# An encoder layer with experts in tiles of 128 rows: a first expert tile made of four experts' first 32 rows, one scatter per tile, six square roots on ScalarE

## The reference

```
h = rms_norm(x, g_mix_norm);  proj = h @ w_in          # latents of q and kv, rotary key, and q, k, v of the second group
o_a = mla_mix(...)      # 8 heads: q and kv expanded from the latents, QK-norm per head, rotary part, dense softmax over 512 keys
o_b = na_mix(...)       # 8 heads: QK-norm, window of 8 x 16 grid points, bias, softmax
x = x + concat(rms_norm(o_a), rms_norm(o_b)) @ w_out
h2 = rms_norm(x, g_ffn_norm)
# hier_moe: group by top 1 of 4, then top 2 of the 4 experts in that group
eid = g_idx * EXPERTS_PER_GROUP + e_idx;  wts = pg_top * pe_top / sum(pe_top)
hid = silu(h2 @ w_gate[e]) * (h2 @ w_up[e]) * combine  # 1024 -> 256, 16 experts
x = x + sum over e of hid @ w_down[e]
```

## Time and profile before

| | us |
|---|---|
| median of 3 runs (lowest, highest) | 523.04 (521.43, 523.22) |
| the profiled execution's own time | 523.25 |
| its span | 521.4 |
| TensorE busy | 466.7 (90%) |
| VectorE, ScalarE, GpSimd busy | 219.9, 146.0, 171.6 |
| last product of the experts ends | 501.5 |

### The profile page before, as it was taken

One profiled execution on the slowest core, in us unless ns is written; L12 is line 12 of the kernel. 1 busy time (PEld: TensorE's weight loads), 2 busy tenths in 40 slices (PEclk: granted clock), 3 DMA queues, 4 the chain that ended last, 5 costly groups with the idle time before them and its releaser, 6 DMA issues. The chain is left out here.

```text
span 521.4 us, 7733 instructions
## 1 busy us (share of the span) xinstructions
PE 466.7 (90%) x2848; PEld 229.7 (44%) x2848; DVE 219.9 (42%) x688; ACT 146.0 (28%) x332; POOL 171.6 (33%) x175
## 2 busy tenths in 40 slices
PE   4999999989999999999999989349999999999940
PEld 2554544444555565554555556233333433333200
DVE  1222864424655645455466666435222332222110
ACT  2301422324554566544353542200111000000100
POOL 1211168878199920000010202300172222222332
PEclk9999999999999999999999999559999999999985
DMA  7999900003300000193000549965899999999312
GB/s 285 431 366 405 370 3 1 1 0 123 140 2 1 0 1 1 30 413 123 1 1 1 202 169 370 394 216 194 296 341 391 393 392 378 372 374 363 72 26 33
DMA packets 29609, 100.05 MB, mean 192 GB/s; under 512 B 5376, under 2 KB 6912, under 8 KB 29184
## 3 DMA queue, kind: packets, MB, share of 16 engines
q1 hardware_dynamic: 21216, 84.04, 41.6%
q0 software_dynamic: 5904, 8.43, 7.0%
q10 hardware_dynamic: 2448, 7.04, 3.6%
HBM read 77.39 MB, written 35.21 MB: 216 GB/s over the span
## 5 line engine op out<-in xcount | busy, mean ns | idle before, releaser
L1301 PE MATMUL bank<-arena 128*128 128x512 f32 (+1 forms) x256 | 112.6, 589 | 2.4 <-DMA arena<-in_w_in_lat 2.4
L1628 PE MATMUL bank<-arena 128*32 128x512 f32 x832 | 92.4, 596 | 0.0
L599 POOL DMA_INDIRECT out<-arena x25 | 38.7, 1549 | 129.5 <-issue 91.3
L1301 PEld LDWEIGHTS bank<-arena 128*128 128x128 f32 x256 | 48.4, 196 | 51.0 <-issue 48.2
L1276 PEld LDWEIGHTS bank<-arena 128*128 128x128 f32 (+1 forms) x380 | 45.6, 141 | 43.3 <-issue 37.7
L1276 PE MATMUL bank<-arena 128*128 128x128 f32 (+1 forms) x380 | 54.6, 277 | 9.3 <-DMA arena<-in_x 4.4
L1474 PE MATMUL bank<-arena 128*128 128x512 f32 x112 | 54.1, 605 | 0.5 <-issue 0.5
L1628 PEld LDWEIGHTS bank<-arena 128*32 128x32 f32 x832 | 25.7, 110 | 57.3 <-issue 57.3
L1648 PE MATMUL bank<-arena 128*32 128x512 f32 x416 | 47.0, 592 | 0.8 <-DVE arena L1220 0.8
L958 DVE COPY arena<-bank 128x512 f32<-128x512 f32 (+2 forms) x64 | 35.8, 582 | 20.9 <-PE bank L1276 20.9
L837 ACT ACTIVATE arena<-bank 128x256 f32<-128x256 f32 x13 | 5.0, 384 | 133.5 <-PE bank L1628 133.5
(11 more groups left out here) (162 smaller groups left out, 509.0 us busy)
## 6 DMA issues: line engine op xcount, KB each, us to landing
arena<-in_w_gu SPq DMA_DIRECT2D x17, 2048.0 KB, 18.2
arena<-in_w_dn SPq DMA_DIRECT2D x17, 1024.0 KB, 18.6
slot_rows<-arena SPq DMA_DIRECT2D x1, 11308.0 KB, 38.2
arena<-slot_rows ACTq DMA_DIRECT2D x13, 514.0 KB, 7.2
arena<-in_w_out SPq DMA_DIRECT2D x2, 2048.0 KB, 8.2
arena<-in_x SPq DMA_DIRECT2D x4, 512.0 KB, 10.8
arena<-in_w_in_k SPq DMA_DIRECT2D x1, 2048.0 KB, 16.4
arena<-in_w_in_q SPq DMA_DIRECT2D x1, 2048.0 KB, 22.5
```

What stands on the lines that cost most here:

```text
L599: nc.gpsimd.indirect_dma_start(out=out_rows, out_offset=bass.IndirectOffsetOnAxis(ap=tag_row[:, g, run:run + 1], axis=0), in_=y_sb[g % 3], ...
L1301: last = nc.tensor.matmul(product_bank(i)[:, 0:width], hT[:, k, t * P:(t + 1) * P], w[:, k, :], start=(k == 0), stop=(k == KD - 1))
L1628: last = nc.tensor.matmul(GU[g % 2][BLK * b:BLK * (b + 1), :], xT[g % 2][:, k, BLK * b:BLK * (b + 1)], w_gu[n % RING][:, k, :], start=(k = ...
```

## The change

**Roots.** The root of the latents, of the four query and key tiles and of `nak` are taken as a square root on ScalarE (`deviation`) and a reciprocal on VectorE. The one of `naq` stays on GpSimd.

**Places.** Experts are renumbered by `PLACES`, so that neighbours belong to different groups. A token's two experts are of one group, so no tile holds a token twice, and each tile takes one scatter.

**The first tile.** Tile 0 now holds 32 rows of each of places 0 to 3, filled from token tiles 0 and 1. If they have fewer than 32 rows there, the rest is padded (`pads`): it counts into the ranks of the later token tiles. The other 64 rows of these four places are tiles 1 and 2. Tile 0 is read back when the rows of token tiles 0 and 1 have landed, and its first product begins before the last token tile's choice is ranked (`counted`). The four stages of tile 0 come before tiles 1 and 2 are turned. Turning and gain of tile 0 are done in ScalarE's copies.

```
-EXTRA = TOP * SEQ // (CAP + 1)
+EARLY = P // BLK
+EXTRA = EARLY + (TOP * SEQ - EARLY * (CAP - BLK + 1)) // (CAP + 1)
+PLACES = [EPG * (n % G) + n // G for n in range(E)]
...
         def loads_of(g):
+            if g < 3:
+                return ([0, 1, 2, 3], [0, 0, 1, 1], [2, 2, 3, 3])[g]
             return [(4 * g + b) // 3 if g < ITEMS else E + g - ITEMS for b in range(4)]
         def last_item(n):
-            return (CAP * n + CAP - 1) // P if n < E else ITEMS + n - E
+            return max(g for g in range(TILES) if n in loads_of(g))
...  (GpSimd)
-                    send(t, k, slots[0], ITEMS, s_disp)
+                    send(t, k, slots[0], ITEMS, s_disp[t // 2])
...
-            for g in range(0, ITEMS, 3):
-                add(g, 0)
...
-                added(g + 1, 1)
-                added(g + 2, 0)
-                add(g + 2, 1)
-            added(LAST - 1, 1)
-            add(LAST, 0)
+            for g in range(ITEMS):
+                if g >= 2:
+                    added(g - 2)
+                add(g)
+                if g < 2:
+                    overflow(2 * g)
+                    overflow(2 * g + 1)
+            added(LAST - 2)
+            added(LAST - 1)
+            add(LAST)
...  (ScalarE)
+            def deviation(key, v):
+                act.wait_ge(s_var, dve_roots.index(key) + 1)
+                nc.scalar.activation(v, v, ACT.Sqrt).then_inc(s_sqrt, 1)
...
             for t in range(T):
                 queries_keys(t)
+                if t > 0:
+                    deviation(("qk", t - 1), flat(rs_qk[:, t - 1]))
             for t in range(2, T):
                 projection("nak", t, nak, NAW)
+            deviation(("qk", T - 1), flat(rs_qk[:, T - 1]))
...
             turned("q", 3)
+            deviation(("nak", 0), flat(rs_na[:, 0]))
...
             h2_rows(T - 1)
+            act.wait_ge(s_disp[0], 16 * TOP * 2)
+            nc.scalar.dma_start(xg[0], x_dram[0:P, :]).then_inc(s_xg[0], 16)
+            for b in range(2):
+                p = turn["early", 0, b]
+                act.wait_ge(s_tp, p + 1)
+                for k in range(4 * b, 4 * b + 4):
+                    last = nc.scalar.activation(xT[0][:, k, :], TPB[p % 2][:, (k - 4 * b) * P:(k - 4 * b + 1) * P], ACT.Copy,
+                                                scale=cols[:, C_FFN + k:C_FFN + k + 1])
+                last.then_inc(s_tpa[p % 2], 1)
             top_exps(T - 1)
...  (VectorE)
             def qk_norm(t):
-                dve.wait_ge(s_root, root["qk", t] + 1)
+                dve.wait_ge(s_sqrt, dve_roots.index(("qk", t)) + 1)
+                link(nc.vector.reciprocal(rs_qk[:, t], rs_qk[:, t]))
...
+                if t == 1:
+                    link(nc.vector.tensor_tensor(pads, konst[:, K_FLOOR:K_FLOOR + E], KB_OF[t][:, 64:64 + E], ALU.subtract))
+                    nc.vector.tensor_scalar(pads, pads, 0.0, None, ALU.max).then_inc(s_pad, 1)
+                nc.vector.scalar_tensor_tensor(early, KB_OF[t][:, 32:32 + E], BLK - 0.5, konst[:, K_LOW:K_LOW + E],
+                                               ALU.is_lt, ALU.mult)
...
             tile_tags(0)
-            x_read(1)
-            tile_tags(1)
             extras_out()
-            for g in range(LAST + 1):
+            hidden(0)
+            hidden_read(0)
+            slots_out()
+            right_y(0)
+            for g in range(1, 3):
+                x_read(g)
+                tile_tags(g)
+            for g in range(1, LAST + 1):
...  (TensorE)
+            for b in range(2):
+                side_turn(("early", 0, b))
+            def counted():
...
-            x_turns(0)
+            gate_up(0, range(2))
+            counted()
+            gate_up(0, range(2, KD))
+            hid_turns(0)
+            down(0)
             x_turns(1)
-            for g in range(LAST + 1):
+            x_turns(2)
+            for g in range(1, LAST + 1):
                 gate_up(g)
-                if g > 0:
+                if g > 1:
                     down(g - 1)
```

More of the change, by code:

```diff
@@ L273, in bank_read @@
             return (s_tpa if act else s_tpe)[p % 2], sum(same)
[L276 removed]
+        roots = [("x", t) for t in range(T)] + [("naq", 0)]
         roots += [("oa", t) for t in range(T)] + [(w, t) for t in range(T) for w in ("ob", "x1")]
@@ L542, in _ @@
             for w, (name, buf) in enumerate((("nak", nak), ("naq", naq))):
-                pool.wait_ge(s_root, root[name, 0] + 1)
+                if w:
+                    pool.wait_ge(s_root, root["naq", 0] + 1)
+                else:
+                    pool.wait_ge(s_nakr, 1)
                 for t in range(T):
@@ L593, in _, with add @@
             pool.wait_ge(s_out, 16 * T)
-            def add(g, run):
+            def add(g):
                 pool.wait_ge(s_ya, g + 1)
@@ L898, in _ @@
             nc.vector.tensor_scalar(rs_lat, rs_lat, EPS, None, ALU.add).then_inc(s_var, 1)
-            dve.wait_ge(s_root, root["lat", 0] + 1)
+            dve.wait_ge(s_sqrt, dve_roots.index(("lat", 0)) + 1)
+            link(nc.vector.reciprocal(rs_lat, rs_lat))
             for t in range(T):
@@ L1047, in ranks_out @@
                 dve.wait_ge(s_cnt, t + 1)
-                link(nc.vector.tensor_tensor(early, slot, over, ALU.add))
+                link(nc.vector.tensor_tensor(early, early, slot, ALU.add))
+                link(nc.vector.tensor_tensor(early, early, over, ALU.add))
                 for k in range(TOP):
@@ L1457, in side_turn @@
                     transposes(key, four(x_sb[:, t, :], b))
+                if kind == "early":
+                    pe.wait_ge(s_xg[0], 16)
+                    transposes(key, four(xg[0], b))
             def out_projection(key, part):
@@ L1614, in x_turns, with gate_up @@
                     last.then_inc(s_tt, 1)
-            def gate_up(g):
-                pe.wait_ge(s_te, turn_x(g, 1) + 1)
-                if g == 0:
-                    pe.wait_ge(s_cnt, T)
-                if g == 1:
-                    pe.wait_ge(s_countr, 1)
-                if g >= 2:
-                    pe.wait_ge(s_hid, g - 1)
-                for n in sorted(set(loads_of(g))):
-                    pe.wait_ge(s_wgu[n % RING], 16 * (n // RING + 1))
-                for k in range(KD):
+            def gate_up(g, steps=range(KD)):
+                if 0 in steps:
+                    if g == 0:
+                        for b in range(2):
+                            pe.wait_ge(*bank_read(turn["early", 0, b]))
+                        pe.wait_ge(s_mx, 2 * MU)
+                    else:
+                        pe.wait_ge(s_te, turn_x(g, 1) + 1)
+                    if g == 1:
+                        pe.wait_ge(s_lgr, T)
+                    if g >= 2:
+                        pe.wait_ge(s_hid, g - 1)
+                    for n in sorted(set(loads_of(g))):
+                        pe.wait_ge(s_wgu[n % RING], 16 * (n // RING + 1))
+                for k in steps:
                     for b, n in enumerate(loads_of(g)):
@@ L1629, in gate_up @@
                                                 w_gu[n % RING][:, k, :], start=(k == 0), stop=(k == KD - 1))
-                last.then_inc(s_gu, 1)
+                if KD - 1 in steps:
+                    last.then_inc(s_gu, 1)
             def hid_turns(g):
```

157 lines of the change are left out of this document (85 added, 72 removed).

## The result

The changed kernel takes 525.38 us (median of 6 runs), the kernel before 522.81 on the same chip: a ratio of 1.006, interval 1.0039 to 1.0082. The forecast was 515.5. The profiled execution of after has a span of 523.3 and an own time of 525.08, against 521.4 and 523.25. Those two differ by 1.83 us, the medians by 2.57.

What follows compares the result with a forecast made beforehand. TensorE, busy 90% of the span, was taken as the bound, with the end set by scatters. 523.25 + 3.9 (roots) - 1.9 (early tile net of weights) - 9.7 (tail) = 515.55, stated as 515.5; range 510.5 to 520.7.

Steps and rivals of the forecast that it cites:

- Part 4, the weights: Expert weights requested later, at 364.5: TensorE waits 2.8 us at tile 10 or one earlier, leaving -1.9 of -4.7.
- Weights lag further: Rival in the expert tiles: scatters come a tile earlier and compete with weights; 3.5 to 5.1 us more, chance 0.17.
- Part 3, the early tile: Gap at 334 to 349: early products fill TensorE's wait on rows; tile 1 starts 1.1 us sooner, tile 2 on 4.7.
- parts 2 and 3: Extra slot-choice work, +0.7 us, included in the early tile's net gains: 1.1 us at tile 1, 4.7 from tile 2.
- Part 1, the roots: Projections to first exponential: ScalarE's copies wait behind roots, a table load is added, normalised-key waits go; +3.9 us.
- The second stall: Before the third key projection: TensorE waits 2 us on ScalarE's copies behind the next root; projection starts at 75.0.
- The first exponential near 130: Sign at the start of attention: ScalarE's first exponential, at 126.13 before, comes near 130; before 127 would refute.
- Part 5, the tail: Kernel's end: one scatter per tile shortens the chain of landings, 5.8 us a hop; end 9.7 us earlier.
- The rival that ended slower: TensorE's lower clock lasts through the early tile, including its second product; 8.9 us more than counted, 524.4, chance 0.07.
- The waits on gate and up weights before tile 9 or 10: Sign in the late expert tiles: TensorE waits 3 us there for gate and up weights.

Runs made afterwards that it cites:

- the late request alone: Kernel before with one scatter per tile and no early tile; expert 5's weights asked for one tile later, with those of expert 6: 517.47 us, 0.9898.
- The halved bytes: Kernel with early tile, single scatter and roots on GpSimd; gate and up weights of experts from 5 on loaded only by half: 510.91 us, 0.9775.
- the reordered requests: Changed kernel with down weights of experts 5 and 6 asked for ahead of gate and up weights of 7 and 8: 522.24 us, 0.9997.

## Why the prediction was wrong

The sum in the profiled execution of before was +3.9, -1.9, -9.7. It came out as +4.3, +6.2, -8.6, which is +1.9 against the measured 1.83 (525.08 less 523.25). The first is the delay of the last h2 rows, the second what the start of the last product adds to it, the third the tail.

**Part 4, the weights: the step that failed.** It read "The weights that tile 10 needs were asked for at 435.75" and worked the bytes out to that one date: 2.8 us of waiting. Its request time was right (364.5, and 369.5 with the 4.3 us and the late start of tile 1). But it looked at one deadline, that which had the least slack before. The idle DMA engines of 358 to 374 moved the tight place forward, to down product 3. There the wait was 8.39, and the lower clock behind it added 1.41: 9.8 in place of 2.8. Three things were left out: the down weights' own date of release (381.34), which puts them behind four larger transfers; scatters and sends that now fall into that very stretch; and the clock after a long wait. How much each of them is worth is known in part: of the 4.4 us by which these down weights landed later than with the late request alone, 1.8 are open. The halved bytes show that the weights are the cause (-10.2 against the same kernel with all bytes), the reordered requests that their order makes up 3 us of it. The rival "Weights lag further" had the direction, with 3.5 to 5.1; it was 7.0 more, and its reason, scatters that come a tile earlier and compete, was a part of it.

**Part 3, the early tile: right.** Tile 1 came 0.5 us sooner and tile 2 3.8, after the 4.3 is taken off (the last h2 rows at 329.87 for the 325.56 of the earlier trace rows), with parts 2 and 3 put at 1.1 and 4.7. The early rows landed at 338.2 (333.9 without the shift, 334.2 foretold).

**Part 1, the roots: right in size, and partly by luck.** ScalarE's copies did wait for the variance, but three details were off. The prediction took the variance of tile 0 as ready at 67.82, as before. It came at 69.38: the last two operations of its sum, 0.18 us each before, took 1.02 and 0.95. They now ran beside GpSimd's squares, which no longer stood behind the power (66.89 to 69.35):

```profile
67.37 1.02 DVE L972 TENSOR_TENSOR small<-small 128x24 f32<-128x24 f32 x1
68.43 0.95 DVE L974 TENSOR_SCALAR small<-small 128x24 f32<-128x24 f32 x1
```

So TensorE stood still for 4.95 and not 3.5. The second stall, 2 us before the third key projection, did not come; in its place the 12 matmuls behind the first took 6.65 for 4.46, as the clock was 0.50 from 67.7 to 74.5. That projection started at 76.75 (75.0 foretold). And with the wait on normalised keys 1.7 us of lower clock behind it went as well (the product at 114.90 took 8.73 for 7.03), which the sum didn't have. These offset each other: the first scores came 3.35 later (3.0). The wait on normalised keys went as foretold. "The first exponential near 130" came at 130.34. The table load costs 1.28 there, and the next instruction starts 0.01 us after it. "ScalarE: Activation LUTs" of the Trainium skill, What ACT_TABLE_LOAD costs, adds a drain to the 1.28; no trace of this case shows one.

**Part 5, the tail: right in kind, 1.1 short.** 8.6 and not 9.7 us. A hop with a whole tile's rows takes 6.65 (508.93 to 515.58), where 5.8 was taken for it, and the scatter of tile 11 starts 0.55 after the start of the last product (508.93 for 508.38), where 0.05 was taken. From the last scatter's start to the end it is 7.7, for 8.0.

**The rival that ended slower** gave 524.4, near the 525.4, but for another reason: its place, the early tile's second product, ran at full clock (3.64 us at 356.66). The clock did stay low longer than counted, to 351.0, so that the six steps from 347.83 took 6.91. That cost nothing, since TensorE would have waited behind them: the wait there is 0.97, and 2.9 in the kernel with roots on GpSimd, whose clock was back at 340.5. In the eight other kernels with the early tile the second product took 4.92 to 5.73 for 3.62, so there this rival's clock did reach that place in part. The waits on gate and up weights before tile 9 or 10 did not come; it was down weights, at tile 3.

## What to carry to other kernels

When a change holds buffers longer, look for the stretch in which the DMA engines then have nothing to fetch, and carry the lost bytes to every later deadline, each transfer with its own release and place in the queue, not only to the deadline that was tightest before. An instruction that waits on a slow chain belongs in its engine's order where that chain is done: four roots of 0.2 us each, moved by a few places, were worth 7.5 us here. And a loss on the busiest engine can be hidden by a slower chain behind it (here two scatters a tile), until that chain is mended; measure parts with the mended chain too. Last, when the profile names an engine for a wait, look whether the program waits for it at all, and when the DMAs that it waits for landed.

## What the chip showed unexpectedly

A stall of 5 to 8 us in TensorE's dense work brought its clock to the lower level while it still stood: the down product behind the 8.4 us wait took 5.03, and 6.29 behind one of 6.0, for 3.62 at 2.4 GHz; the 12 query matmuls behind 4.95 took 6.65 for 4.46. The time behind a stall was thus 1.4 to 2.7 us longer, and the shorter wait cost more behind it: when the 8.4 us wait ended at 409.59, 2.8 us of low clock were left (to 412.4), and 5.3 when the one of 6.0 ended at 401.97 (to 407.3). In both the loss is half of what was left.

Two small VectorE operations took five times as long beside GpSimd's squares as without them (1.02 and 0.95 us for 0.18). And nearly full DMA engines moved 379 GB/s with weights and row reads alone, 302 with GpSimd's scatter and sends among them.
